# A two-layer hybrid transformer trunk: the even layer's probability-value products as f32r passes of high and low parts

## The chip, the cores and the metric

The kernel runs on one core of a Trainium2 chip. The metric is the device time of one execution in microseconds (us): 1273.81 us before, the median of 3 runs (1273.42 to 1273.93).

## What is computed

A decoder trunk of two layers over 512 tokens of width 1024, all in float32, then a final RMSNorm. Each layer is a mixer and a gated MLP, each behind an RMSNorm and with a residual. The change touches only the mixer of the even layer (layer 0), which has two head groups. Cut to what matters:

```
# A: 4 heads, each with two 64-wide q/k maps (c = 0, 1) and one 128-wide value
s = einsum('bqhcd,bkhcd->bhcqk', q * scale, k)
e, den = masked_exp(s, causal)                 # exp(s - row maximum), row sums
o = einsum('bhcqk,bkhe->bqhce', e, v) / den
o_a = o[c=0] - lam * o[c=1]                    # then an RMSNorm over the 128 values

# B: 8 heads of 64, three (window, dilation) branches combined by their softmax sums;
# here as one softmax in which every key is weighted by the number of branches that see it
o_b = einsum('bhqk,bkhd->bqhd', e * count, v) / sum(e * count)
```

The 1024 columns of o_a and o_b together go into one output projection.

## The kernel before, in words

**Number format of the large products.** A float32 operand is split in a high part of type f32r (a rounded copy, made by ScalarE) and a low part (the operand minus the high part, made by VectorE or GpSimd), and a product is three f32r passes: high by high, high by low, low by high. The weights come in 101 tiles of 128x2048, two buffers (`w_raw`, `w_hi`, `w_lo`); each is loaded by SyncE, copied to `w_hi` by ScalarE (L369), and its `w_lo` is made by VectorE (L773) in the even mixer and by GpSimd (L290) after it.

**The even mixer** runs in 8 groups: g = 0 to 3 are the A heads (a loop), g = 4 to 7 are pairs of B heads (unrolled). The 384 columns of q, k and v of a group lie in `y` (part of the buffer `region`), the value in the last 128 of them. A group has 8 units k = 0 to 7: `i = k // 2` is the block of 128 queries, `m = k % 2` the map or head, and `w = 128 * (i + 1)` the number of keys. A unit passes through four engines:

- TensorE: scores into PSUM bank m (L1421 and L1422, f32r, then a mask, L1424 or L1426);
- VectorE: the negated row maximum (`max_unit`, L881);
- ScalarE: exp into `probs` (`exp_unit`, L491 or L494), which lies in `xn`;
- VectorE, in B only: the weights of the keys and their sum (`weigh_unit`, L887);
- TensorE: transposes of 128x128 into PSUM bank 2 + m (`turn_probs`, L1392);
- ScalarE: the copy into `probsT` (`copy_turned`, L502), also in `xn`;
- TensorE: the product with the values (`values`, L1408), i + 1 float32 matmuls of 128 columns in A and 64 in B, into bank 6 or 7;
- VectorE: after two units, division by the sums and the way out (`heads_out`: L893 to L900 in A, L893 and L904 in B).

**The order** is written out by hand, and each engine runs its instructions in that order. Iteration k of `attention_ab` on TensorE holds: scores of unit k, a piece of the projection of the next group (`part`, L1365, 12 matmuls of 384 columns; for k = 0 and 2 to 7 and at the end of the group, none at k = 1 and 8), transposes of unit k - 1, values of unit k - 2. At k = 9 stand the transposes of the next group's q and k (L1355), then the values of unit 7. In group 7 there is no next group: pieces of the output projection (L1332) stand in iterations 0, 2, 3, 4, 5 and 7. VectorE runs, in iteration k: maximum of unit k; at k = 4, 6, 8 `heads_out`; from k = 4 to 7 an addition to the next group's q, k, v (`add_part`, L856); in B `weigh_unit`; at k = 1 a whole weight tile's low part (L773), and at k = 5 another; in groups 4 to 6, at the end of some iterations, `between`, which holds the A heads' norm (`sub_norm`, four L1088). After iteration 8 it makes the low parts of the next q and k (`head_lows`, L840 and L843) and runs the last `heads_out`. GpSimd rotates q and k of the next group (L314 to L320).

Of the kernel before, what the change touches and what calls it, by code (L numbers as in the profile page):

```python
# [21 lines left out]
NT = SEQ // 128  # L22
# [31 lines left out]
def trunk_program(nc, x_in, weights, consts, masks, vectors, gains, out):  # L54
# [5 lines left out]
    with ExitStack() as ctx:  # L60
# [28 lines left out]

        xn = sb("xn", [128, 2, DM])  # L90
        probs = xn[:, 0, :].rearrange("p (a n) -> p a n", a=2)
# [41 lines left out]
        first_lo = nc.alloc_sbuf_tensor_at("first_lo", [128, 4, SEQ], f32r, offset=region_at + 4 * (12288 + 4 * SEQ))  # L133
        masks_f32 = region[:, 12288:12288 + M_END]
        split_at = region_at + 4 * (12288 + M_END)
# [21 lines left out]
        pT_ready, pT_copied, pv_ready, o_ready = sem("pT_ready"), sem("pT_copied"), sem("pv_ready"), sem("o_ready")  # L157
        conv_started, conv_done, silu_ready = [[sem(f"{n}{l}") for l in range(2)] for n in
# [204 lines left out]
        def _(sc):  # L363
# [133 lines left out]
            def copy_turned(g, k):  # L497
# [4 lines left out]
                sc.activation(probsT[:, m, 0:w], ps[:, 2 + m, 0:w], ACT.Copy).then_inc(pT_copied, 1)  # L502

            def attention_ab(kind, g, more):

                for k in range(9):
                    if k == 0 and more:
                        copy_low(g + 1, 1, 5)
                    if k < 8:
                        exp_unit(kind, g, k)  # L510
                    if k >= 1:
                        copy_turned(g, k - 1)
# [23 lines left out]
            def attention_c(h, g):  # L536
# [5 lines left out]
                for k in range(9):  # L542
# [4 lines left out]
                    if k >= 1:  # L547
                        copy_turned(g, k - 1)
# [189 lines left out]
        def _(ve):  # L738
# [138 lines left out]

            def max_unit(g, k):
# [11 lines left out]
            def heads_out(kind, h, g, i):  # L890
# [12 lines left out]
                elif kind == "B":  # L903
                    ve.tensor_tensor(y[:, i, ds(384 * g, 128)].rearrange("p (m d) -> p m d", m=2),  # L904
                                     bank[:, 0:128].rearrange("p (m d) -> p m d", m=2),
                                     rden[:, 2 * i:2 * i + 2].unsqueeze(2).broadcast_to([128, 2, 64]),
                                     ALU.mult).then_inc(o_ready, 1)
# [288 lines left out]
        def _(pe):  # L1196
# [186 lines left out]
            def turn_probs(kind, g, k):  # L1383
# [5 lines left out]
                if k >= 2:  # L1389
                    pe.wait_ge(pT_copied, 8 * g + k - 1)  # L1390
# [462 lines left out]
```

## Time and profile before

| | |
|---|---|
| median of 3 runs | 1273.81 us (1273.42 to 1273.93) |
| the profiled execution, its own time | 1273.91 us |
| its span in the trace | 1272.1 us |
| busy share of TensorE (matmul), VectorE, ScalarE, GpSimd | 97%, 40%, 39%, 45% |
| granted clock of TensorE, mean | 0.998 of 2.4 GHz |

The profiled execution is 1.8 us longer than its span, which is what lies around the span, and 0.1 us above the median. The even mixer's attention groups run from 44 to about 280 us. In the profile, PE is TensorE's matmul side and PEld its weight loads; a group starts with the first `L1421` matmul of 128 columns. These starts lie at 44.02, 73.20, 102.53, 131.88, 161.22, 192.09, 221.63 and 252.50 us, so that an A group takes 29.3 us and a B group 29.5 to 30.9 us. A float32 matmul shows as two records in the trace, an f32r or bf16 matmul or a transpose as one.

### The profile page before, as it was taken

Reading aid. Unit: us, or ns where it says so; the run is one execution under the profiler, and the core shown is the slowest. Engines: PE = TensorE matmul, PEld = TensorE weight load, DVE = VectorE, ACT = ScalarE, POOL = GpSimd, SP = SyncE. Lnnn points to the kernel's source line nnn. Section 1 sums busy time; section 2 is a strip of 40 time slices with the busy share of each in tenths; the row PEclk is TensorE's granted clock in tenths of the full one; section 3 lists DMA queues with packets and bytes.
Section 4 is the critical chain, followed back from the end, with each engine's and each line's share of the span. In section 5 each row is a group of like instructions: output and inputs, shape, how many; then the busy total and the mean of one; then the engine's idle time right before and its main releaser. Section 6 shows DMA issues by size and latency. Waiting matters only on the chain.

```text
span 1272.1 us, 17211 instructions
## 1 busy us (share of the span) xinstructions
PE 1232.1 (97%) x6376; PEld 1055.9 (83%) x6376; DVE 506.2 (40%) x885; ACT 494.0 (39%) x702; POOL 566.6 (45%) x501
## 2 busy tenths in 40 slices
PE   5999999999999999999999999999999999999996
PEld 5999989888888888888878879878888888888885
DVE  6665577755212112132324165634522121222324
ACT  4455545544323222243334255443523232343332
POOL 1344444414344444466644441611444444456662
PEclk9999999999999999999999999999999999999999
DMA  7221111112222222222223211210222222222221
GB/s 267 94 81 66 66 67 67 67 67 83 100 99 99 99 99 92 98 75 99 99 99 102 81 67 67 99 67 34 86 97 98 99 99 99 99 99 98 87 80 66
DMA packets 17036, 114.75 MB, mean 90 GB/s; under 512 B 1888, under 2 KB 2016, under 8 KB 4064
## 3 DMA queue, kind: packets, MB, share of 16 engines
q1 hardware_dynamic: 16128, 110.99, 23.9%
q10 hardware_dynamic: 864, 3.15, 0.8%
q8 instruction: 31, 0.51, 0.2%
q14 instruction: 13, 0.11, 0.0%
HBM read 112.03 MB, written 2.10 MB: 90 GB/s over the span
## 4 chain that ended last, share of the span: by engine, by line
issue 38%; POOL 30%; PE 24%; DVE 5%; ACT 2%; DMA 1%; POOLq 0%; DVEq 0%; ACTq 0%
POOL w_lo L290 30%; PE ps L1365 7%; PE ps L1633 2%; PE ps L1277 2%; PE ps L1408 2%; PE ps L1613 2%; PE ps L1557 2%; PE ps L1243 1%; PE ps L1392 1%; DVE w_lo L773 1%; PE ps L1287 1%; PE ps L1355 1%; PE ps L1258 1%; PE ps L1696 1%; ACT tmp L419 1%
## 5 line engine op out<-in xcount | busy, mean ns | idle before, releaser
L290 POOL TENSOR_TENSOR w_lo<-w_raw,w_hi 128x512 fp32r<-128x512 f32 (+1 forms) x326 | 457.3, 1434 | 535.5 <-ACT w_hi L369 476.6
L369 ACT ACTIVATE w_hi<-w_raw 128x2048 fp32r<-128x2048 f32 x96 | 183.7, 1913 | 313.7 <-PE ps L1287 155.2
L1287 PE MATMUL ps<-hT_hi,w_hi 128*128 128x512 f32 x688 | 267.7, 389 | 0.0
L1287 PE MATMUL ps<-hT_hi,w_lo 128*128 128x512 f32 x688 | 267.7, 389 | 0.0
L1287 PE MATMUL ps<-hT_lo,w_hi 128*128 128x512 f32 x688 | 267.6, 389 | 0.0
L1287 PEld LDWEIGHTS ps<-hT_lo,w_hi 128*128 128x128 f32 x688 | 129.2, 188 | 27.0
L1287 PEld LDWEIGHTS ps<-hT_hi,w_lo 128*128 128x128 f32 x688 | 129.2, 188 | 26.8
L1287 PEld LDWEIGHTS ps<-hT_hi,w_hi 128*128 128x128 f32 x688 | 129.2, 188 | 26.4
L1002 DVE TENSOR_TENSOR hT_lo<-region,hT_hi 128x2048 fp32r<-128x2048 f32 (+1 forms) x22 | 58.5, 2668 | 144.4 <-ACT hT_hi L584 144.4
L972 DVE SCALAR_TENSOR_TENSOR qk<-ps,vec,qk 128x511 f32<-128x511 f32 x44 | 33.0, 750 | 202.9 <-ACT qk L558 202.9
L558 ACT ACTIVATE qk<-ps,vec 128x512 f32<-128x512 f32 x44 | 34.3, 780 | 178.4 <-PE ps L1287 166.3
L1527 PE MATMUL ps<-w_hi,hT_hi 128*128 128x512 f32 x256 | 99.6, 389 | 0.0
L1527 PE MATMUL ps<-w_lo,hT_hi 128*128 128x512 f32 x256 | 99.6, 389 | 0.0
L1527 PE MATMUL ps<-w_hi,hT_lo 128*128 128x512 f32 x256 | 99.6, 389 | 0.0
L982 DVE TENSOR_TENSOR region<-ps,qk 128x512 f32 (+1 forms) x44 | 30.4, 691 | 155.4 <-PE ps L1287 155.4
L314 POOL TENSOR_TENSOR tmp<-region,cst 128x256 f32<-128x256 f32 x30 | 23.4, 780 | 143.5 <-DVE region L856 115.8
L1365 PE MATMUL ps<-w_hi,hT_hi 128*128 128x384 f32 x224 | 80.6, 360 | 1.4 <-ACT region L483 1.0
L1365 PE MATMUL ps<-w_hi,hT_lo 128*128 128x384 f32 x224 | 75.2, 336 | 0.0
L1365 PE MATMUL ps<-w_lo,hT_hi 128*128 128x384 f32 x224 | 74.0, 335 | 0.4 <-DVE w_lo L773 0.4
L881 DVE TENSOR_REDUCE neg_max<-ps 128x1 f32<-128x128 f32 (+3 forms) x80 | 39.1, 489 | 44.0 <-PE ps L1426 20.8
L1527 PEld LDWEIGHTS ps<-w_lo,hT_hi 128*128 128x128 f32 x256 | 48.1, 188 | 10.0
L1527 PEld LDWEIGHTS ps<-w_hi,hT_hi 128*128 128x128 f32 x256 | 48.1, 188 | 10.0
(212 smaller groups left out, 2194.7 us busy)
## 6 DMA issues: line engine op xcount, KB each, us to landing
w_raw<-weights SPq DMA_DIRECT2D x101, 1024.0 KB, 4.8
gain<-gains ACTq DMA_DIRECT2D x5, 512.0 KB, 3.6
out<-region SPq DMA_DIRECT2D x4, 512.0 KB, 2.6
x<-x_in SPq DMA_DIRECT2D x3, 512.0 KB, 10.9
cst<-consts SPq DMA_DIRECT2D x1, 640.0 KB, 12.7
x<-x_in ACTq DMA_DIRECT2D x1, 512.0 KB, 6.6
region<-masks SPq DMA_DIRECT2D x1, 384.0 KB, 13.3
vec<-vectors SPq DMA_DIRECT2D x1, 282.5 KB, 12.9
```

The lines of the kernel that those rows point to most:

```text
L290: ins = pool.tensor_tensor(w_lo[:, slot, cols], w_raw[:, slot, cols], w_hi[:, slot, cols].bitcast(f32), ALU.subtract)
L369: sc.activation(w_hi[:, slot, :], w_raw[:, slot, :], ACT.Copy).then_inc(w_hi_ready, 1)
L558: sc.activation(qk[:, s, :], ps[:, s, :], ACT.Identity, scale=vec[:, ds(8 * i + (col + 2), 1)], bias=vec[:, ds(8 * i + (col + 3), 1)]).the ...
L881: ve.tensor_reduce(neg_max[:, k:k + 1], ps[:, m, 0:w], AX.X, ALU.max, negate=True).then_inc(max_ready, 1)
L972: own.link(ve.scalar_tensor_tensor(qk[:, s, 1:SEQ], ps[:, s, 0:SEQ - 1], vec[:, ds(8 * i + (col + 1), 1)], qk[:, s, 1:SEQ], ALU.mult, ALU. ...
L982: ve.tensor_tensor(act[:, ds(2 * i + s, 1), :], ps[:, 2 + s:3 + s, :], qk[:, 2 + s:3 + s, :], ALU.mult).then_inc(val_bank_free[l], 1)
L1002: ve.tensor_tensor(hT_lo[:, places, :], act[:, ds(kt, count), :], hT_hi[:, places, :].bitcast(f32), ALU.subtract).then_inc(act_lo[l], count)
L1277: ins = pe.matmul(ps[:, banks[t], 0:width], h[:, k0 + k, t * 128:(t + 1) * 128], w[:, slot, k * width:(k + 1) * width], start=first and k ...
L1287: ins = pe.matmul(bank, w[:, slot, k * pitch + 128 * s:k * pitch + 128 * s + 128], h[:, k:k + 1, :], start=k == 0 and n == 0, stop=k == KT ...
L1365: ins = pe.matmul(ps[:, bank, 0:384], h_[:, 4 * half + k, t * 128:(t + 1) * 128], w_[:, half, k * 384:(k + 1) * 384], start=first and k == ...
L1408: ins = pe.matmul(o, probsT[:, m, b * 128:(b + 1) * 128], v, start=b == 0, stop=b == i)
L1527: ins = pe.matmul(ps[:, 4 * c + t, :], a[:, t * 128:(t + 1) * 128], w[:, slot, u * 512:(u + 1) * 512], start=first and u == units[0] and n ...
```

## The change

In groups 0 to 7 the transposed probabilities and the values are split in high and low parts, and their product runs as f32r matmuls:

- ScalarE copies a group's values to the high half of a new buffer `v_split` (`value_highs`, one instruction of 512 columns after the exp of unit 0). VectorE makes the low half (`value_lows`, one instruction of 512 columns) in iteration 1, ahead of the weight tile.
- ScalarE's copy of the transposed probabilities goes to `probsT_hi`, of type f32r, in the same place and with the same length. VectorE makes `probsT_lo` (`low_turned`) from PSUM and `probsT_hi`, one instruction of w columns for each unit: unit k - 2 in iteration k behind `max_unit`, and unit 7 ahead of `head_lows`. It lies in `stage`.
- In A, a block takes three matmuls of 128 columns in place of one float32 matmul. In B it takes one of 128 columns (high probabilities by high and low values, side by side) and one of 64 (low by high), in place of one float32 matmul of 64.
- In B, `heads_out` multiplies both halves by the inverse sums and adds them: three instructions for one, each behind the one before.
- The values of unit k - 2 now wait for `pT_low` (the low part) and no longer for `pT_copied`; those of unit 0 also for `v_ready`. The transposes of unit k wait for the low part of unit k - 2.
- `q_split`, `k_high` and `k_low` move up by 256 columns to make room.

```diff
+            def value_highs(g):
+
+                v = y[:, :, ds(384 * g + 256, 128)].rearrange("p t (m d) -> p t m d", m=2)
+                sc.activation(v_split[:, :, :, 0, :], v, ACT.Copy).then_inc(v_high, 1)
...
                     if k < 8:
                         exp_unit(kind, g, k)
+                    if k == 0:
+                        value_highs(g)
...
+            def value_lows(g):
+
+                v = y[:, :, ds(384 * g + 256, 128)].rearrange("p t (m d) -> p t m d", m=2)
+                ve.wait_ge(v_high, g + 1)
+                ve.tensor_tensor(v_split[:, :, :, 1, :], v, v_split[:, :, :, 0, :].bitcast(f32), ALU.subtract)\
+                  .then_inc(v_ready, 1)
...
+                    o = y[:, i, ds(384 * g, 128)].rearrange("p (m d) -> p m d", m=2)
+                    both = bank[:, 0:256].rearrange("p (m h d) -> p m h d", m=2, h=2)
+                    r = rden[:, 2 * i:2 * i + 2].unsqueeze(2).broadcast_to([128, 2, 64])
+                    low = o_tmp[:, :].rearrange("p (m d) -> p m d", m=2)
+                    own.link(ve.tensor_tensor(low, both[:, :, 1, :], r, ALU.mult))
+                    own.link(ve.tensor_tensor(o, both[:, :, 0, :], r, ALU.mult))
+                    ve.tensor_tensor(o, o, low, ALU.add).then_inc(o_ready, 1)
...
+            def low_turned(g, k):
+                i, m, w = unit(k)
+                ve.wait_ge(pT_copied, 8 * g + k + 1)
+                ve.tensor_tensor(probsT_lo[:, m, 0:w], ps[:, 2 + m, 0:w], probsT_hi[:, m, 0:w].bitcast(f32),
+                                 ALU.subtract).then_inc(pT_low, 1)
...
                     if k < 8:
                         max_unit(g, k)
+                    if k >= 2:
+                        low_turned(g, k - 2)
...
                     if k == 1:
+                        value_lows(g)
                         split_lo(2 * g + 3, 1)
...
+                low_turned(g, 7)
...
+                    pe.wait_ge(pT_low, 8 * g + k + 1)
+                    if k == 0:
+                        pe.wait_ge(v_ready, g + 1)
...
                     if kind == "A":
-                        v, o = y[:, b, ds(384 * g + 256, 128)], ps[:, 6 + i % 2, 128 * m:128 * m + 128]
...
+                        pe.matmul(o, hi, v_split[:, b, :, 0, :], start=b == 0, stop=False)
+                        pe.matmul(o, hi, v_split[:, b, :, 1, :], start=False, stop=False)
+                        ins = pe.matmul(o, lo, v_split[:, b, :, 0, :], start=False, stop=b == i)
+                        continue
+                    if kind == "B":
+                        pe.matmul(o, hi, v_split[:, b, m, :, :], start=b == 0, stop=False)
+                        ins = pe.matmul(o[:, 0:64], lo, v_split[:, b, m, 0, :], start=False, stop=b == i)
+                        continue
```

TensorE, group 0, iteration 2, from the transpose of unit 1 to the scores of unit 3. `xn` holds the probabilities, `cst` the identity. Before:

```order
L1392 MATMUL ps<-cst,xn 128x128
L1408 ISA
L1408 MATMUL ps<-region,xn 128x128
```

After:

```order
L1426 MATMUL ps<-cst,xn 128x128
L1436 REGISTER_ALU
L1443 MATMUL ps<-v_split,probsT_hi 128x128
L1444 MATMUL ps<-v_split,probsT_hi 128x128
L1445 MATMUL ps<-v_split,probsT_lo 128x128
```

One float32 matmul became three f32r matmuls, at the same place in the row.

VectorE, the start of an A group (the maxima of units 0 and 1, the weight tile of iteration 1, the maximum of unit 2). Before:

```order
L881 TENSOR_REDUCE neg_max<-ps 128x1
L880 REGISTER_ALU
L881 TENSOR_REDUCE neg_max<-ps 128x1
L772 ISA
L773 TENSOR_TENSOR w_lo<-w_raw,w_hi 128x2048
L880 REGISTER_ALU
L881 TENSOR_REDUCE neg_max<-ps 128x1
```

After:

```order
L902 TENSOR_REDUCE neg_max<-ps 128x1
L895 REGISTER_ALU
L896 ISA
L896 TENSOR_TENSOR v_split<-region,v_split 128x8x64
L786 ISA
L787 TENSOR_TENSOR w_lo<-w_raw,w_hi 128x2048
L901 REGISTER_ALU
L902 TENSOR_REDUCE neg_max<-ps 128x1
L941 TENSOR_TENSOR probsT_lo<-ps,probsT_hi 128x128
```

(The after piece starts with the maximum of unit 1.) The low part of unit 0, for which TensorE's first values wait, stands behind the value lows, the weight tile and the maximum of unit 2.

VectorE, a B group, from the weight tile of iteration 5 to the addition of iteration 6. Before:

```order
L773 TENSOR_TENSOR w_lo<-w_raw,w_hi 128x2048
L881 TENSOR_REDUCE neg_max<-ps 128x1
L893 RECIPROCAL rden<-den 128x2
L904 TENSOR_TENSOR region<-ps,rden 128x128
L856 TENSOR_TENSOR region<-region,ps 128x384
```

After:

```order
L787 TENSOR_TENSOR w_lo<-w_raw,w_hi 128x2048
L902 TENSOR_REDUCE neg_max<-ps 128x1
L941 TENSOR_TENSOR probsT_lo<-ps,probsT_hi 128x384
L914 RECIPROCAL rden<-den 128x2
L929 TENSOR_TENSOR o_tmp<-ps,rden 128x128
L930 TENSOR_TENSOR region<-ps,rden 128x128
L931 TENSOR_TENSOR region<-region,o_tmp 128x128
L870 TENSOR_TENSOR region<-region,ps 128x384
```

Three instructions more stand in this iteration ahead of the addition and of `weigh_unit`.

## Rows read from the trace of the kernel before

**Rows 1.** The page: busy time of engines; then tenths in 40 slices.

```profile
PE 1232.1 (97%) x6376; PEld 1055.9 (83%) x6376; DVE 506.2 (40%) x885; ACT 494.0 (39%) x702; POOL 566.6 (45%) x501
...
DVE  6665577755212112132324165634522121222324
```

**Rows 2.** Stretches of one A and one B group: length, busy time by engine.

```profile
103.00:134.00 31.00, 30.40 (x203) 28.78 (x203) 19.14 (x43) 16.58 (x36) 12.84 (x20) 1.00 0.18 68
...
192.00:219.00 27.00, 26.58 (x178) 24.69 (x177) 20.01 (x47) 12.09 (x23) 14.46 (x20) 1.00 0.22 79
```

**Rows 3.** Timeline, PE: start, duration; values of unit 6, then what follows; A, B.

```profile
97.14 1.06 PE L1408 MATMUL ps<-region,xn 128*128 x8
98.04 1.15 PE L1355 MATMUL ps<-cst,qk 128*128 128x128 f32 x9
...
216.01 1.00 PE L1408 MATMUL ps<-region,xn 128*128 128x64 f32 x8
216.85 1.15 PE L1355 MATMUL ps<-cst,qk 128*128 128x128 f32 x9
```

**Rows 4.** Timeline, group 0: f32r scores of 128 columns, and a weight load (PEld).

```profile
46.88 0.22 PE L1421 MATMUL ps<-k_high,q_split 128*128 128x128 f32 x1
46.94 0.27 PE L1422 MATMUL ps<-k_low,q_split 128*128 128x128 f32 x1
47.05 0.23 PE L1426 MATMUL ps<-mask_bf,ident_bf 128*128 128x128 bf16 x1
...
46.88 0.19 PEld L1422 LDWEIGHTS ps<-k_low,q_split 128*128 128x128 f32 x1
```

**Rows 5.** Timeline, group 1, iterations 0 to 2: DVE, ACT and PE.

```profile
76.03 0.29 DVE L881 TENSOR_REDUCE neg_max<-ps 128x1 f32<-128x128 f32 x1 [0.19 <-PE ps L1426]
76.24 2.28 DVE L773 TENSOR_TENSOR w_lo<-w_raw,w_hi 128x2048 fp32r<-128x2048 f32 x1
78.44 0.42 DVE L881 TENSOR_REDUCE neg_max<-ps 128x1 f32<-128x256 f32 x1
...
76.36 0.37 ACT L494 ACTIVATE xn<-ps,neg_max 128x128 f32<-128x128 f32 x1
...
76.39 0.33 PE L1392 MATMUL ps<-cst,xn 128*128 128x128 f32 x1 [0.39 <-ACT xn L494]
...
79.11 0.39 PE L1408 MATMUL ps<-region,xn 128*128 x2
```

**Rows 6.** Durations: ACT copy and DVE operations of 512, 512, 384 and 128 columns.

```profile
L502 ACT ACTIVATE xn<-ps 128x512 f32<-128x512 f32 x12 | 7.2, 598 | 8.8 <-PE ps L1392 8.8
...
L843 DVE TENSOR_TENSOR k_low<-ps,k_high 128x512 fp32r<-128x512 f32 x4 | 2.8, 692 | 0.1
L856 DVE TENSOR_TENSOR region<-region,ps 128x384 f32<-128x384 f32 x12 | 6.5, 544 | 0.0
L904 DVE TENSOR_TENSOR region<-ps,rden 128x128 f32<-128x128 f32 x10 | 2.9, 291 | 0.3
```

**Rows 7.** Timeline, group 4, iteration 1 and 2: the weight tile and the values of unit 0.

```profile
165.31 2.29 DVE L773 TENSOR_TENSOR w_lo<-w_raw,w_hi 128x2048 fp32r<-128x2048 f32 x1
...
167.26 0.33 PE L1408 MATMUL ps<-region,xn 128*128 128x64 f32 x2
```

**Rows 8.** Timeline, group 4, iterations 6 to 8: the norm, its followers, TensorE.

```profile
183.80 0.68 DVE L881 TENSOR_REDUCE neg_max<-ps 128x1 f32<-128x512 f32 x1
...
184.49 0.78 PE L1408 MATMUL ps<-region,xn 128*128 128x64 f32 x6
186.46 0.66 PE L1392 MATMUL ps<-cst,xn 128*128 128x128 f32 x4 [1.19 <-DVE xn L887]
```

**Rows 9.** Timeline, group 5, end of iteration 7: the norm of 128x128, four times.

```profile
214.66 2.47 DVE L1088 SCALAR_TENSOR_TENSOR region<-region,rstd,sub_gain 128x128 f32<-128x128 f32 x4
217.06 0.15 DVE L893 RECIPROCAL rden<-den 128x2 f32<-128x2 f32 x1
```

**Rows 10.** Timeline, group 7: iteration 6, then iteration 8 and 9.

```profile
271.79 0.69 DVE L881 TENSOR_REDUCE neg_max<-ps 128x1 f32<-128x512 f32 x1 [1.22 <-PE ps L1424]
271.92 0.78 PE L1408 MATMUL ps<-region,xn 128*128 128x64 f32 x6
277.57 1.96 PE L1408 MATMUL ps<-region,xn 128*128 128x64 f32 x16
277.77 0.60 ACT L502 ACTIVATE xn<-ps 128x512 f32<-128x512 f32 x1 [0.46 <-PE ps L1392]
```

**Rows 11.** Waits of PE from 67 to 162 us: in total, times, longest.

```profile
PE ps L1392 <- ACT xn L494: 1.2, 3, 0.4
```

More of the change, by code:

```diff
@@ L133, in trunk_program @@
         first_lo = nc.alloc_sbuf_tensor_at("first_lo", [128, 4, SEQ], f32r, offset=region_at + 4 * (12288 + 4 * SEQ))
+        probsT_hi = nc.alloc_sbuf_tensor_at("probsT_hi", [128, 2, SEQ], f32r, offset=xn_at + 4 * DM)
+        probsT_lo = nc.alloc_sbuf_tensor_at("probsT_lo", [128, 2, SEQ], f32r, offset=stage_at)
         masks_f32 = region[:, 12288:12288 + M_END]
-        split_at = region_at + 4 * (12288 + M_END)
+        v_split = nc.alloc_sbuf_tensor_at("v_split", [128, NT, 2, 2, 64], f32r, offset=region_at + 4 * 12288)
+        split_at = region_at + 4 * (12288 + 1024)
         q_split, k_high, k_low = (nc.alloc_sbuf_tensor_at(n, [128, 2, SEQ], f32r, offset=split_at + 4 * 2 * SEQ * j)
@@ L501, in copy_turned @@
                     sc.wait_ge(pv_ready, 8 * g + k - 1)
-                sc.activation(probsT[:, m, 0:w], ps[:, 2 + m, 0:w], ACT.Copy).then_inc(pT_copied, 1)
+                dst = probsT if kind == "C" else probsT_hi
+                sc.activation(dst[:, m, 0:w], ps[:, 2 + m, 0:w], ACT.Copy).then_inc(pT_copied, 1)
+            def value_highs(g):
+                v = y[:, :, ds(384 * g + 256, 128)].rearrange("p t (m d) -> p t m d", m=2)
+                sc.activation(v_split[:, :, :, 0, :], v, ACT.Copy).then_inc(v_high, 1)
             def attention_ab(kind, g, more):
@@ L547, in attention_c @@
                     if k >= 1:
[L548 removed]
+                        copy_turned("C", g, k - 1)
             def mlp(l, n0):
@@ L1389, in turn_probs @@
                 if k >= 2:
-                    pe.wait_ge(pT_copied, 8 * g + k - 1)
+                    pe.wait_ge(*((pT_copied, 8 * g + k - 1) if kind == "C" else (pT_low, 8 * g + k - 1)))
                 for b in range(i + 1):
@@ L1396, in values @@
                 i, m, w = unit(k)
-                pe.wait_ge(pT_copied, 8 * g + k + 1)
+                if kind == "C":
+                    pe.wait_ge(pT_copied, 8 * g + k + 1)
+                else:
+                    pe.wait_ge(pT_low, 8 * g + k + 1)
+                    if k == 0:
+                        pe.wait_ge(v_ready, g + 1)
                 if i >= 2 and m == 0:
                     pe.wait_ge(o_ready, 4 * g + i - 1)
+                o = ps[:, 6 + i % 2, 128 * m:128 * m + 128]
                 for b in range(i + 1):
+                    hi, lo = (p[:, m, b * 128:(b + 1) * 128] for p in (probsT_hi, probsT_lo))
                     if kind == "A":
-                        v, o = y[:, b, ds(384 * g + 256, 128)], ps[:, 6 + i % 2, 128 * m:128 * m + 128]
-                    elif kind == "B":
-                        v, o = y[:, b, ds(384 * g + (256 + 64 * m), 64)], ps[:, 6 + i % 2, 64 * m:64 * m + 64]
+                        pe.matmul(o, hi, v_split[:, b, :, 0, :], start=b == 0, stop=False)
[6 more added lines that the diff above has]
+                        continue
                     else:
```

11 lines of the change are left out of this document (5 added, 6 removed).

## The prediction, made before the result

> **What bounds the kernel now.** I read the page's busy shares first, then its 40 slices, then the timelines of single groups. TensorE is busy 97% of the span; VectorE is busy 40% on average, but 6 to 7 tenths in slices 1 to 9, which are the attention groups this change touches [rows 1]. A 31 us stretch of the A groups has 19.1 us of VectorE work, a 27 us stretch of B has 20.0 us [rows 2]. So TensorE sets the time, and VectorE has over a third of its time free in A and a quarter in B. The question is then twofold: how long the new value products are on TensorE, and whether a low part from VectorE is there when TensorE comes to the values. Where it isn't, TensorE waits, since nothing else stands in its row.
>
> **TensorE, A groups.** Each of the 80 blocks (4 groups, 20 blocks each) has one float32 matmul, two records, and gets three f32r matmuls. The 8 records of unit 6 start at 97.14 and what follows starts at 98.04, which is 0.90/8 = 0.11 us a record [rows 3]. What does an f32r matmul of 128 columns take? The trace has no long run of them. It has pairs: the first starts at 46.88, the second at 46.94, the mask's at 47.05 [rows 4]. The first follows in 0.06 us and has its weights loaded already; the second takes 0.11 us, and its weight load starts only at 46.88, with the first matmul. In B, a float32 record has half the columns (64) and still takes (216.85 - 216.01)/8 = 0.105 us [rows 3]. A record that doesn't shrink with its columns is bound by something that every record has, and that is the weight load. All new matmuls load weights of 128x128, so I take 0.11 us for each, with 0.085 (the mean of the pair, 0.17/2) and 0.06 as the cheaper bounds. A: 240 x 0.11 - 160 x 0.11 = +8.8 us.
>
> **TensorE, B groups.** 80 blocks had two records and get two f32r matmuls (128 and 64 columns). 160 x 0.11 - 160 x 0.105 = +0.8 us; I take +0.5, since the narrow ones may keep 0.105.
>
> The Trainium skill, in "TensorE: Matmul & The Clock Gate", section "Back-to-back issue gap", gives about 81 ns a matmul of 128 columns in a stream with weight loads. That speaks against my 0.11, and by it A would be 240 x 0.081 - 17.6 = +1.8 and B 160 x 0.081 - 16.8 = -3.8, a TensorE sum of -2.0 in place of +9.3. No row here shows a run at that rate.
>
> **What of it is given back.** At the start of groups 1 to 4 TensorE waits 0.4 to 0.5 us for the first exp or its weighting, since VectorE is still busy with the last `heads_out` (0.39 in group 1, 1.2 in all for three groups) [rows 5, 11]. The longer values of unit 7 (12 records for 8, +0.44) lie ahead of this wait and fill it: -1.6 us for four groups. TensorE's sum is +8.8 + 0.5 - 1.6 = +7.7 us.
>
> **The first values of each group.** This is the largest wait that the change adds. In iteration 1 VectorE ran the maximum of unit 1 (76.03), the weight tile (76.24) and the maximum of unit 2 (78.44) [rows 5]. Now, in group 1: ScalarE, free at 76.36 where it started the second exp, makes the value highs first (0.62 us, by the copy of 512 columns at 0.60) and is done at about 77.0 [rows 5, 6]. VectorE waits for that, makes the value lows until 77.6 (0.60 from start to start, by the 0.69 of `k_low` less 0.08 of overlap), the weight tile until 79.8 (2.2), the maximum of unit 2 until 80.2, then the low part of unit 0 (0.29) [rows 6]: ready at 80.5. TensorE used to start these values at 79.11 [rows 5]. It waits 1.4 us. The second exp comes 0.6 us later, but its transposes stand behind a `part` of 2.1 us, which hides that. In B it is the same with other numbers: the tile started at 165.31, the value lows push it to 165.9, so the low part is there at 168.8, against values at 167.26 [rows 7]: 1.5 us. There are 4 x 1.4 + 4 x 1.5 = +11.6 us. This wait can't be less than 0.8 us a group (no value lows in the way, 6.4 us in all) unless VectorE does the low part ahead of the tile, which its order excludes.
>
> **Later values of A.** Behind a `part` of 2.1 us the low part (maximum 0.6 and low 0.6 at most) is hidden. Iteration 8 has no `part`: the values of unit 6 stand behind one set of transposes (0.45) and the longer values of unit 5, and need copy plus low part, 0.60 + 0.69. I take 0.1 a group, +0.5 us.
>
> **Later values of B.** VectorE gets, from k = 4 to the weighting of unit 7, low parts of 256, 256, 384 and 384 columns (0.35 + 0.35 + 0.47 + 0.47) and two `heads_out` that have three chained instructions for one of 0.29 (+0.7 each) [rows 6]: 3.0 us of work. The groups have about 2 us of idle VectorE there, partly ahead of the tile of k = 5. What doesn't fit shows on TensorE:
> - Group 4: the norm ends at 183.80, then come the maximum and the low part of unit 5 (0.6 + 0.56), ready at 185.0 even with no lag, against values at 184.49; TensorE waits 1.19 us already for the weighting of unit 7 [rows 8], and that comes 1.6 us later. +1.7 us for the two.
> - Group 5: the norm of 2.47 us at the end of iteration 7 delayed nobody before. Now the low part of unit 6 stands behind it: 217.06 + 0.69 + 0.05 = 217.8, against values at 216.01 [rows 3, 9]. That is 1.8 us; with 0.8 of lag carried over, +2.6 us.
> - Group 6: iteration 8 alone, +0.5 us.
> - Group 7: iteration 6 has no piece of projection. The maximum of unit 6 starts at 271.79, so the low part of unit 4 is ready at about 273.0, against 271.92: 1.05 us. In iteration 8 and 9 the last 16 records ran without a gap from 277.57, while the copy of unit 7 started at 277.77 [rows 10]; now VectorE's low part of unit 6, a `heads_out`, an addition and the low part of unit 7 (0.61 + 1.1 + 0.6 + 0.69) stand in the way, 0.5 + 1.4 us. +3.0 us.
>
> That is +7.8 us for B.
>
> ScalarE's part adds nothing beyond the above: its copies keep their length, and the value highs are counted. SyncE, GpSimd and the DMAs issue what they did before; what stands behind the attention is shifted as a whole.
>
> **Sum.** 7.7 + 11.6 + 0.5 + 7.8 = +27.6 us on the profiled execution's 1273.9 (0.1 above the median): **1301.5 us**, 2.2% slower.
>
> **Rivals.**
> - *Cheap f32r matmuls.* If a record takes the pair's mean of 0.085, A loses 240 x 0.025 = 6.0 us of its cost, B 160 x 0.025 = 4.0 us, of which TensorE returns some by waiting longer for the same low parts (half in B, I estimate): -8.0, so 1293.5 us. For it: the pair. Against it: the 0.11 of the second and of the records of 64 columns. The skill's 81 ns would come out about here too.
> - *VectorE becomes the bound of B.* A B group of 27 us has 20.0 us of VectorE work; the change adds 3.7 (low parts), 0.6 and 4 x 0.7, which is 27.1. If its chained waits don't overlap with TensorE's pieces at all, groups 4 to 7 each lose 3 us more: 1313 us.
> - *The low parts are hidden.* Then only TensorE's records count: 1273.9 + 7.7 = 1281.6 us. It needs VectorE to be 1.4 us ahead in iteration 2, and the start at 78.44 right behind the tile says it is not.
> - *Faster than before.* If f32r records ran at 0.06, as the first of the pair does, A is 240 x 0.06 - 17.6 = -3.2 and B 160 x 0.06 - 16.8 = -7.2, together -10.4 us: 1263.5 us. It decides for faster only if all new waits together stay under 10 us, and I count 19.9.
> - *It does nothing measurable.* The new work would have to fall where TensorE idles; it idles 0.39 us ahead of the first transposes of an A group [rows 5], against 2.2 us of new records in it.
>
> **Chances.** Forecast (1296 to 1308) 0.64; cheap matmuls 0.15; VectorE-bound B 0.12; low parts hidden 0.05; faster 0.02; no change 0.02. The range goes from 1290 (cheap matmuls with their bound) to 1311 (most of the VectorE case). A measurement of this kernel tells about 0.2%, 2.5 us, from no change. So faster 0.02, same 0.02, slower 0.96.
>
> **What would show it.** Right: A groups about 32 us from start to start (29.3 before) and B groups 31 to 34; TensorE idle ahead of the first values of every group by 1.4 to 1.5 us, released by the low part; 0.11 us between starts of value records, 80 records more in all. VectorE at 8 tenths or more in the slices of the B groups, and in group 5 the low part of unit 6 right behind the norm. Wrong: no idle ahead of values in iteration 2, value records at 0.06 to 0.09 us, or waits in A in iterations 3 to 7, where I have none.

## The result, and the profile after

The changed kernel takes 1306.26 us (median of 4 runs, 1305.94 to 1308.97), against 1273.62 us of the kernel before: a ratio of 1.026, 95% interval 1.025 to 1.028. It is 32.6 us slower. The forecast was 1301.5 us, in a range from 1290 to 1311. The profiled execution of the changed kernel took 1308.97 us with a span of 1307.2, which is 35.1 us more than the span before. So what follows explains 35.1 us for the profile, and 32.6 for the median.

The page of the changed kernel, against [rows 1]; `PEclk` is the granted clock in tenths of 2.4 GHz, in 40 slices of 32.7 us:

```profile
PE 1252.3 (96%) x6452; PEld 1072.3 (82%) x6456; DVE 544.7 (42%) x989; ACT 498.3 (38%) x710; POOL 566.0 (43%) x501
...
DVE  6766677786521212132325046644522222232324
...
PEclk9999998899999999999999999999999999999999
```

TensorE has about the 80 records more that the change makes (6452 for 6376; a few records can be missing from a trace), VectorE 38.5 us more work, and two slices show an 8 where the kernel before had a 9 in all 40. The span grew by 35 us, TensorE's busy time by 20. The rest is waiting, and TensorE's waits over the whole span name its releaser (waited for: us in total, times, longest):

```profile
PE ps L1448 <- DVE probsT_lo L941: 12.4, 13, 1.8
PE ps L1443 <- DVE probsT_lo L941: 5.0, 4, 1.3
...
PE ps L1338 <- DVE region L870: 1.5, 1, 1.5
```

L941 is `low_turned`, L1443 and L1448 are the first value matmuls of a block in A and in B: 17.4 us in 17 waits, none of which the kernel before had. This is the mechanism of the forecast. Here is its first place, group 1, where [rows 5] showed the kernel before (DVE, then PE):

```profile
79.90 0.69 DVE L896 TENSOR_TENSOR v_split<-region,v_split 128x512 fp32r<-128x512 f32 x1 [0.23 <-ACT v_split L514]
80.50 2.29 DVE L787 TENSOR_TENSOR w_lo<-w_raw,w_hi 128x2048 fp32r<-128x2048 f32 x1
82.71 0.42 DVE L902 TENSOR_REDUCE neg_max<-ps 128x1 f32<-128x256 f32 x1
83.04 0.28 DVE L941 TENSOR_TENSOR probsT_lo<-ps,probsT_hi 128x128 fp32r<-128x128 f32 x1
...
83.45 0.32 PE L1443 MATMUL ps<-v_split,probsT_hi 128*128 128x128 f32 x1 [1.29 <-DVE probsT_lo L941]
83.61 0.27 PE L1444 MATMUL ps<-v_split,probsT_hi 128*128 128x128 f32 x1
83.72 0.27 PE L1445 MATMUL ps<-v_split,probsT_lo 128*128 128x128 f32 x1
83.83 0.33 PE L1467 MATMUL ps<-k_high,q_split 128*128 128x256 f32 x1
```

Value lows, weight tile, maximum, low part: four instructions in a row without a gap, and TensorE idle for 1.29 us until the last of them ends. The second and third value matmul start 0.11 us apart, where [rows 3] had 0.11 for a float32 record. The delay is longer than the idle time shown: the scores of unit 3 (83.83) start 7.29 us after the group's start here and 5.76 us after it in the run of the TensorE half below, which has the same records and no such wait. That is 1.53 us for a wait of 1.29.

Not all of it is waiting. The profile shows four stretches in which the granted clock is low. These are windows of the changed kernel (length, busy time of PE, PEld, DVE, ACT and POOL, then the granted clock as a share of 2.4 GHz, DMA share, GB/s):

```profile
202.00:208.00 6.00, 6.00 (x37) 5.82 (x37) 3.66 (x9) 3.36 (x7) 2.34 (x5) 0.72 0.00 0
216.00:222.00 6.00, 5.42 (x24) 5.00 (x24) 3.06 (x12) 1.78 (x6) 0.00 (x0) 0.72 0.46 175
240.00:248.00 8.00, 8.00 (x39) 8.00 (x39) 4.53 (x11) 4.55 (x6) 0.03 (x1) 0.57 0.00 1
312.00:318.00 6.00, 5.91 (x29) 5.52 (x30) 3.15 (x8) 1.79 (x3) 0.00 (x0) 0.72 0.00 0
```

In their middle, windows of 2 us show 0.50, the lower of the two levels, 1.2 GHz. The clock takes 6 x 0.28 us three times and 8 x 0.43 us once there, 8.5 us, if all of TensorE's work in them is stretched by it. In the kernel before, no window of 2 us between 44 and 280 us was under 0.99. One such place on PE, the end of group 5:

```profile
239.99 0.24 PE L1449 MATMUL ps<-v_split,probsT_lo 128*128 128x64 f32 x1
240.07 1.85 PE L1389 MATMUL ps<-cst,qk 128*128 128x128 f32 x12
241.57 0.46 PE L1448 MATMUL ps<-v_split,probsT_hi 128*128 128x128 f32 x1
241.82 0.36 PE L1449 MATMUL ps<-v_split,probsT_lo 128*128 128x64 f32 x1
242.00 0.45 PE L1448 MATMUL ps<-v_split,probsT_hi 128*128 128x128 f32 x1
```

A pair of value matmuls takes 0.43 us there (241.57 to 242.00), twice the 0.22 us of the pairs before 240. The clock fell about 2 us after the end of the longest wait of the group, 1.80 us ahead of 239.16: the window from 241 to 242 us is the first under 1.00, with 0.57.

The starts of groups 0 to 7 are now at 43.75, 76.54, 109.14, 141.71, 174.28, 209.33, 247.26 and 281.65 us, and the output projection that follows group 7 begins at 319.70 (284.37 before):

| group | before, us | after, us | more | of it at low clock | left | forecast |
|---|---|---|---|---|---|---|
| 0 to 3 (A), sum | 117.2 | 130.5 | 13.3 | 0 | 13.3 | 13.7 |
| 4 | 30.9 | 35.1 | 4.2 | 1.7 | 2.5 | 2.8 |
| 5 | 29.5 | 37.9 | 8.4 | 5.1 | 3.3 | 4.1 |
| 6 | 30.9 | 34.4 | 3.5 | 0 | 3.5 | 2.0 |
| 7 | 31.9 | 38.1 | 6.2 | 1.7 | 4.5 | 4.5 |

(The column "forecast" splits its 27.6 us by group. The 0.5 us for B's records is left out of it. The group starts are 0.3 us earlier than before, so the column "more" adds up to 35.6 us, and "left" to 27.1.)

### The profile page after: what moved, and what is told of

Its sections match the earlier page's. It is cut to its first block, busy times and chain, and to the rows that moved or that the text cites. A ratio compares the mean times of both kernels' runs of the same rounds, so it can differ in the third digit from the quotient of the medians.

```text
span 1307.2 us, 17487 instructions
## 1 busy us (share of the span) xinstructions
PE 1252.3 (96%) x6452; PEld 1072.3 (82%) x6456; DVE 544.7 (42%) x989; ACT 498.3 (38%) x710; POOL 566.0 (43%) x501
## 4 chain that ended last, share of the span: by engine, by line
issue 37%; POOL 29%; PE 22%; DVE 7%; ACT 3%; DMA 0%; POOLq 0%; DVEq 0%; ACTq 0%
POOL w_lo L296 29%; PE ps L1399 6%; DVE w_lo L787 2%; PE ps L1679 2%; PE ps L1311 2%; PE ps L1659 2%; PE ps L1603 1%; PE ps L1277 1%; PE ps L1389 1%; PE ps L1321 1%; PE ps L1426 1%; PE ps L1292 1%; DVE neg_max L902 1%; ACT tmp L425 1%; PE ps L1443 1%
## 5 line engine op out<-in xcount | busy, mean ns | idle before, releaser
L1321 PEld LDWEIGHTS ps<-hT_hi,w_hi 128*128 128x128 f32 x688 | 129.2, 188 | 26.6
L320 POOL TENSOR_TENSOR tmp<-region,cst 128x256 f32<-128x256 f32 x30 | 24.8, 828 | 172.9 <-DVE region L870 145.4
## 6 DMA issues: line engine op xcount, KB each, us to landing
region<-masks SPq DMA_DIRECT2D x1, 384.0 KB, 13.3
```

What stands on the lines that cost most here:

```text
L1321: ins = pe.matmul(bank, w[:, slot, k * pitch + 128 * s:k * pitch + 128 * s + 128], h[:, k:k + 1, :], start=k == 0 and n == 0, stop=k == KT ...
```

## The experiments

Two theories were tested. **Theory 1** is the forecast's: TensorE pays for 80 more records and waits for low parts that stand too far back in VectorE's row. **Theory 2** was formed on the result: the idle stretches of TensorE make the chip grant the half clock for a few microseconds afterwards, which costs time on top of the idle time itself. The kernel before was run beside each set: 1273.4 us with the first four runs, 1274.2 with the next four, 1273.8 with the last two.

### One half of the change at a time

TensorE's half: the same f32r matmuls, all on high parts, with no low part made or waited for.

```diff
-                    pe.wait_ge(pT_low, 8 * g + k + 1)
+                    pe.wait_ge(pT_copied, 8 * g + k + 1)
...
-                        pe.matmul(o, hi, v_split[:, b, :, 1, :], start=False, stop=False)
+                        pe.matmul(o, hi, v_split[:, b, :, 0, :], start=False, stop=False)
...
-                    if k >= 2:
-                        low_turned(g, k - 2)
```

> The TensorE half of the change alone: the value products run as the same number of f32r matmuls of the same shapes (three of 128 columns in A, one of 128 and one of 64 in B), but all on high parts; VectorE makes no low parts of probabilities or values and takes B's output in one instruction as before, and TensorE waits for ScalarE's copy only. Left out of the computation: every low part of these products. Theory 1 (a record costs 0.11 us, given by the weight load; 7.7 us net): 1281 us (1279 to 1284), granted clock 0.998 as before, no wait at the values. Rival (the pair's mean, 0.085 us a record): 1272 to 1274 us. Rival on the whole result (f32r value products are what costs 33 us, by whatever way): near 1306 us.

Measured: 1281.2 us (1279.6 to 1282.6), ratio 1.006 (1.004 to 1.007). Theory 1's 1281 is met; 0.085 us a record is out. Its A groups take 30.8 us, 1.5 more than before (group 0: 1.9), and groups 5 and 6 take 29.5 and 30.9, exactly as before: B's records cost nothing. What it doesn't show as expected is the clock. In the profiled execution the wait of group 4 that the kernel before has as well [rows 8] is followed by a low stretch (PE, and a window):

```profile
191.95 0.66 PE L1419 MATMUL ps<-cst,xn 128*128 128x128 f32 x4 [1.26 <-DVE xn L908]
...
192.00:202.00 10.00, 10.00 (x53) 10.00 (x54) 3.73 (x9) 5.95 (x10) 1.75 (x4) 0.66 0.01 2
```

That is 3.4 us lost. By their mean clock two of its four executions had it (0.995, 1282.5 and 1282.6 us; the former is the profiled one), two had not (0.998 and 0.997, 1279.6 and 1279.9). So the half as such is worth about 6 us, and the clock adds 3 in some executions.

VectorE's and ScalarE's half: all low parts and the longer B output are made, but the product is the float32 one and doesn't wait for them.

```diff
-                dst = probsT if kind == "C" else probsT_hi
+                dst = probsT
...
-                    pe.wait_ge(pT_low, 8 * g + k + 1)
+                    pe.wait_ge(pT_copied, 8 * g + k + 1)
...
-                        pe.matmul(o, hi, v_split[:, b, m, :, :], start=b == 0, stop=False)
-                        ins = pe.matmul(o[:, 0:64], lo, v_split[:, b, m, 0, :], start=False, stop=b == i)
+                        v, o = y[:, b, ds(384 * g + (256 + 64 * m), 64)], ps[:, 6 + i % 2, 128 * m:128 * m + 64]
...
+                        pe.wait_ge(pT_low, 8 * g + 7)
                         turn_qk(g + 1)
```

> The VectorE and ScalarE half alone: low parts of probabilities and values are made at the same places, B's output takes its three instructions, but the product is the float32 one of before and doesn't wait for a low part (only the transposes that overwrite a PSUM bank do, two units later, and the next group's q and k transposes do for unit 6). The output takes the float32 product and so has a wrong low half added in B. Theory 1 (what costs is that TensorE's values wait for the low part): little of the 33 us shows, 1276 to 1281 us, from maxima, weights and q/k transposes that come later in B, clock near 0.998. Rival (VectorE as such is the bound, with or without that wait): 1290 us or more.

Measured: 1282.1 us, ratio 1.007 (1.005 to 1.009), 1 us above the expected range and far from the rival's 1290. The two halves cost 7.8 and 8.7 us, 16.5 together, and the whole costs 32.9. Half of the cost is in neither of them: it is in the wait that joins them and in the clock. VectorE's half alone still delays TensorE a little in several places (between 44 and 330 us; the first row is the transposes, waiting for B's weighting, the second a `part` whose weight tile comes later, the third a wait for the low part ahead of the next group's transposes, added for this run):

```profile
PE ps L1426 <- DVE xn L908: 2.4, 3, 1.5
PE ps L1399 <- DVE w_lo L787: 2.3, 6, 0.7
...
PE ps L1389 <- DVE probsT_lo L941: 1.1, 1, 1.1
```

### Weight loads or columns

The TensorE half again, with an A block as one matmul of 256 columns and one of 128, so that 384 columns are streamed with two weight loads and not three.

```diff
-                        pe.matmul(o, hi, v_split[:, b, :, 0, :], start=b == 0, stop=False)
-                        pe.matmul(o, hi, v_split[:, b, :, 0, :], start=False, stop=False)
-                        ins = pe.matmul(o, lo, v_split[:, b, :, 0, :], start=False, stop=b == i)
+                        o = ps[:, 6 + i % 2, 256 * m:256 * m + 256]
+                        both = v_split[:, b:b + 1, :, 0, :].broadcast_to([128, 2, 2, 64])
+                        pe.matmul(o, hi, both, start=b == 0, stop=False)
+                        ins = pe.matmul(o[:, 0:128], lo, v_split[:, b, :, 0, :], start=False, stop=b == i)
```

> As the run of the TensorE half alone (no low parts, no wait for them), but an A block takes two f32r matmuls in place of three: one of 256 columns and one of 128. The columns streamed are the same 384; only the number of records, and so of weight loads, falls by 80, to that of the kernel before. Left out: all low parts. Theory 1 (a record costs its weight load, 0.11 us, up to about 200 columns): the cost in A goes away, 1274 to 1277 us against 1281 with three. Rival (the columns or the type cost, not the records): 1280 to 1282 us.

Measured: 1274.7 us (10 runs), ratio 1.0007 (0.9997 to 1.0017): no difference from the kernel before. Its A groups take 29.2 to 29.4 us. Five of the executions, at a mean clock of 0.997 or 0.998, took 1273.7 to 1274.3 us; the other five, at 0.996, took 1275.1 to 1276.1. The profiled one is among the latter, and its clock falls at 187.6 us, behind the wait of group 4 that the kernel before has too. So at full clock nothing is left of the 6 us. The columns and the type cost nothing, the 80 records did. PE, group 0, values of unit 6, then PEld, the weight loads of these matmuls:

```profile
67.74 0.33 PE L1438 MATMUL ps<-v_split,probsT_hi 128*128 128x256 f32 x1
67.91 0.22 PE L1439 MATMUL ps<-v_split,probsT_hi 128*128 128x128 f32 x1
67.97 0.34 PE L1438 MATMUL ps<-v_split,probsT_hi 128*128 128x256 f32 x1
68.14 0.23 PE L1439 MATMUL ps<-v_split,probsT_hi 128*128 128x128 f32 x1
...
67.69 0.19 PEld L1438 LDWEIGHTS ps<-v_split,probsT_hi 128*128 128x128 f32 x1
67.79 0.19 PEld L1439 LDWEIGHTS ps<-v_split,probsT_hi 128*128 128x128 f32 x1
67.92 0.19 PEld L1438 LDWEIGHTS ps<-v_split,probsT_hi 128*128 128x128 f32 x1
68.02 0.19 PEld L1439 LDWEIGHTS ps<-v_split,probsT_hi 128*128 128x128 f32 x1
```

A pair takes 0.23 us (67.74 to 67.97), as two float32 records did; three f32r matmuls of 128 columns took 0.33. Note that the 128-column matmul is followed after 0.06 us, as the first of the pair in [rows 4] was, and the 256-column one after 0.17. The weight loads start 0.10 to 0.13 us apart whatever the columns, and 0.11 apart in the changed kernel too (97.26, 97.37, 97.48 us and so on, in group 1): their spacing, and not the columns, gives the 0.23 of a pair. A start-to-start time of one matmul says little here; the sum over a repeated pattern does. A fixed cost of a matmul other than its weight load would look the same, and no run tells the two apart. Nor does a run show at how many columns the columns begin to count; the 384 of a `part` matmul take 0.17 us.

### The wait at the first values

The whole change, with the low part of unit 0 ahead of the weight tile.

```diff
-                    if k >= 2:
+                    if k >= 3:
                         low_turned(g, k - 2)
...
                         value_lows(g)
+                        low_turned(g, 0)
                         split_lo(2 * g + 3, 1)
```

> The whole change, but in each group the low part of unit 0 is made ahead of the weight tile of iteration 1, not behind it and the maximum of unit 2. Nothing is left out. Theory 1: the wait of 1.2 to 1.8 us at the first values is gone in all 8 groups (10.9 us in the changed kernel's trace), and 2 us come back elsewhere since the tile ends later: about 9 us less, 1297 us; and if such waits are what takes the clock down in B, some of the four stretches at 1.2 GHz go as well, 1291 to 1297 us. Rival (VectorE has no time for it, the wait only moves): within 3 us of 1306.

Measured: 1298.3 us (1295.6 to 1299.1), ratio 1.019 (1.018 to 1.021): 8 us faster than the change. Theory 1 had about 9, and 1291 to 1297 us, so the result is 1 us above its range and outside the rival's, within 3 us of 1306. The waits for L941 fell from 17.4 to 5.9 us, all of them in B, and 3.5 us came back as the wait for the weight tile that now ends later:

```profile
PE ps L1449 <- DVE probsT_lo L941: 5.9, 7, 1.9
PE ps L1400 <- DVE w_lo L787: 3.5, 7, 0.9
```

Three low stretches remained, with 5.1 us lost; the run without most of that clock loss (0.996) took 1295.6 us, those at 0.992 1299.0.

### The norms

The whole change, with two norms of the A heads moved to where no low part of unit 5 or 6 stands behind them.

```diff
-            between = {4: {3: lambda: refine(0, 16), 6: lambda: sub_norm(0)}, 5: {3: lambda: sub_norm(1), 7: lambda: sub_norm(2)},
+            between = {4: {3: lambda: refine(0, 16), 8: lambda: sub_norm(0)}, 5: {3: lambda: sub_norm(1), 8: lambda: sub_norm(2)},
```

> The whole change, with two of the four norms of the A heads moved on VectorE: from the end of iteration 6 of group 4 and of iteration 7 of group 5 to the end of iteration 8 of the same groups, so that the low parts of units 5 and 6 no longer stand behind them. Nothing is left out. Theory 1: the wait of 1.8 us in group 5 and of 1.0 us in group 4 fall to 0.5 us each, and with the former the longest stretch at 1.2 GHz (7 us, 3.4 lost) may go: 1300 to 1305 us. Rival (the norm only pushes the next group's q/k low parts or first maxima): within 1 us of 1306.

Measured: 1306.1 us (1304.4 to 1306.3). The rival's number came, though not by its way. In the profiled execution (1304.4 us) groups 4 and 5 take 33.5 us each (35.1 and 37.9 in the change), 6.0 us less together: 5.1 of it is the clock, which didn't fall there, and 0.9 the waits. The 1.80 us ahead of unit 6's values in group 5 became 0.34, with 0.73 ahead of unit 7's. But the end of group 7 had a longer stretch at half clock, from 306 to 313 us, 3.4 us lost, where the change had lost 1.7. The other three executions had a lower mean clock still (0.993) and took 1.7 us more. At equal clock little is left of the gain: 1306.0 to 1306.3 us at 0.993 here, 1306.5 us at 0.993 in the change.

Both orders together:

> The whole change with both orders: the low part of unit 0 ahead of the weight tile (as in the run that made it 8 us faster), and the two norms at the end of iteration 8. Nothing is left out. Theory 1: the two gains add where they are apart, 1291 to 1296 us, still far above 1273.4, since TensorE's records (+6 to +8 us) and B's VectorE work stay.

Measured: 1295.3 us (1294.5 to 1297.3), ratio 1.017 (1.015 to 1.019): within the range, 3 us below the run with the low part alone, and 21 us above the kernel before. One low stretch remained in its profile.

### The clock

The whole change with work in the waits of B: bf16 matmuls of constants into an unused part of the PSUM bank, placed in TensorE's row ahead of the values that wait longest.

```diff
+                fill = 0 if kind != "B" else {(4, 5): 7, (5, 6): 13, (7, 4): 6, (7, 7): 8}.get((g, k), 9 if k == 0 else 0)
+                for _ in range(fill):
+                    pe.matmul(ps[:, 6 + i % 2, 256:512], ident_bf[:, :], mask_bf[:, M_DIL:M_DIL + 256], start=True, stop=True)
```

> The whole change, with bf16 matmuls of 256 columns of constants into an unused part of the PSUM bank put in TensorE's row in the B groups, ahead of the values that wait 1 us or more: 9 ahead of unit 0 of groups 4 to 7, 7 ahead of unit 5 of group 4, 13 ahead of unit 6 of group 5, 6 and 8 ahead of units 4 and 7 of group 7. They fill the waits with work and shorten none. Theory 2 (TensorE's idle stretches make the chip grant half the clock, four stretches with 8.5 us lost): the clock stays at 1.0 throughout, and the time falls to 1297 to 1301 us although work was added. Rival (the clock falls for another reason, or costs nothing because TensorE waits anyway): 1306 us or more.

Measured: 1302.0 us (1301.0 to 1302.7), 4 us less than the change, with 70 matmuls more, and 1 us above the range that theory 2 gave. No window of 2 us under 0.99 is left in the attention of the profiled execution; three of the four executions had a mean clock of 0.998, the slowest 0.996. Windows of this kernel around three of the four places where the clock fell in the change:

```profile
200.00:214.00 14.00, 13.54 (x98) 12.61 (x97) 11.02 (x28) 8.40 (x15) 4.11 (x7) 1.00 0.00 1
214.00:224.00 10.00, 9.10 (x60) 8.04 (x59) 7.65 (x23) 4.53 (x8) 1.48 (x3) 1.00 0.26 105
236.00:252.00 16.00, 14.81 (x106) 14.01 (x105) 12.36 (x33) 7.58 (x15) 1.80 (x4) 1.00 0.11 36
```

Groups 4 and 5 take 33.6 and 33.5 us (35.1 and 37.9). So theory 2 holds: the fall of the clock comes from TensorE's idle stretches, and what the clock cost can be had back by useless work. From the start of group 4 to the output projection the profiled executions differ by 7.9 us (145.4 and 137.5), close to the 8.5 at stake. As wholes they differ by 7.0 (1308.97 and 1301.96), the medians by 4.3: the other three executions of the change had a mean clock of 0.993 or 0.994 and had lost less.

Is it idleness alone, or idleness together with the small f32r matmuls? The changed kernel with all its waits and float32 products:

```diff
-                dst = probsT if kind == "C" else probsT_hi
+                dst = probsT
...
-                        pe.matmul(o, hi, v_split[:, b, m, :, :], start=b == 0, stop=False)
-                        ins = pe.matmul(o[:, 0:64], lo, v_split[:, b, m, 0, :], start=False, stop=b == i)
+                        v, o = y[:, b, ds(384 * g + (256 + 64 * m), 64)], ps[:, 6 + i % 2, 128 * m:128 * m + 64]
```

> The changed kernel with all its VectorE and ScalarE work and with the values still waiting for their low part, but the product itself the float32 one of before. It leaves the low parts out of the product, and B's low half is wrong. It tells two theories of the clock apart. Theory 2a (TensorE's idle stretches alone take the clock down): waits are those of the changed kernel, so four or so stretches at 1.2 GHz appear, clock 0.992 to 0.995, and the time is 1306 less the 6 us of new records in A: 1299 to 1301 us. Theory 2b (it takes idle stretches together with the small f32r matmuls, which stream 64 or 128 columns of one pass for each weight load where a float32 record streams two passes' worth): the clock stays at 0.998, and the time is 1291 to 1295 us.

Measured: 1301.7 us (1299.1 to 1303.8), at a clock of 0.993 to 0.997; theory 2a had 1299 to 1301, theory 2b 1291 to 1295. Low stretches appear with float32 products too (two in the profile, 1.7 us lost in each), so the waits are enough without f32r value products, as theory 2a had it. The faster executions have the higher clock: 0.997 at 1299.1, 0.996 at 1301.3, 0.993 at 1302.2 and 1303.8. TensorE waited for L941 19.0 us in this kernel, more than in the change, since shorter records arrive earlier:

```profile
PE ps L1447 <- DVE probsT_lo L941: 19.0, 21, 1.8
```

It also shows that the terms don't add: with the waits in place, f32r records cost 4 to 5 us and not 7.8. In the A groups, where no clock falls, they cost 0.9 us a group (32.6 against 31.7), where they cost 1.5 without the waits. That the low stretches are fewer here than in the change could be the type or chance; the runs don't settle it.

The best order and the matmuls of constants together:

> The low part of unit 0 ahead of the weight tile, and bf16 matmuls of constants in the four waits of B that remain (7 ahead of unit 5 of group 4, 13 ahead of unit 6 of group 5, 6 and 8 ahead of units 4 and 7 of group 7). Nothing is left out. Theory 2: the three low-clock stretches of the run without filler (4.5 us lost) go, 1293 to 1295 us at a clock of 0.998. Rival: no change against 1298, or slower by the filler.

Measured: 1293.0 us (1292.6 to 1293.3), the best form of the whole change that was run, and the steadiest: all four executions at 0.997, none of them slower than 1293.3, and no low stretch in the attention of the profiled one. It is theory 2's 1293 to 1295. It is still 1.5% slower than the kernel before.

### TensorE's records against VectorE's time in A

The best form with the wide A product, whose high and low results lie in separate columns and are added by VectorE.

```diff
+                    own.link(ve.tensor_scalar(o_sum[:, :], bank[:, 384:512], rden[:, 2 * i + 1:2 * i + 2], neg_lam[:, :],
+                                              ALU.mult, ALU.mult))
+                    own.link(ve.scalar_tensor_tensor(o_sum[:, :], bank[:, 128:256], rden[:, 2 * i:2 * i + 1],
+                                                     o_sum[:, :], ALU.mult, ALU.add))
...
+                    own.link(ve.tensor_tensor(o, o, o_sum[:, :], ALU.add))
```

> The whole change in the best form so far (low part of unit 0 first, matmuls of constants in four waits of B) with A's product as one matmul of 256 and one of 128 columns, and so with high and low results in separate columns that VectorE adds in the A groups: three instructions more in each of 16 outputs. Nothing is left out. If VectorE has room in A (20 of 31 us busy before), it gains TensorE's 4 to 6 us, 1287 to 1289 us. If the longer output pushes maxima and low parts in A, as in B, it gives the gain back or more: 1293 to 1300 us. I hold the second for likelier.

Measured: 1306.1 us (1305.7 to 1306.3), clock 0.998. It loses 13 us against the run before, where TensorE had 6 to gain, and is 6 us above the worse of the two expected ranges. A groups take 34.2 to 35.2 us (31.6 without), and TensorE waits for `add_part` (L871), which now stands behind the longer output, before it may reuse a bank:

```profile
PE ps L1406 <- DVE region L871: 9.0, 8, 1.5
PE ps L1454 <- DVE probsT_lo L947: 4.8, 8, 0.9
...
103.00:134.00 31.00, 27.37 (x177) 25.50 (x178) 22.88 (x52) 15.26 (x34) 10.24 (x16) 1.00 0.13 38
```

VectorE is busy 22.9 of 31 us here, 19.1 in [rows 2]: a quarter of it is free, and it still sets the pace, as TensorE's waits for it show. That this is so because its instructions are chained and stand in one row is argued, not tested.

## Why the prediction was right, and where it was not

The direction and the mechanism came as forecast: the value records on TensorE, and its waits for low parts that stand too far back in VectorE's row. The terms follow one by one.

- **TensorE's records, +7.7 us.** Measured by themselves: 7.8 us in the median, of which about 1.5 is clock, so 6. The 0.11 us a record is right (three in 0.33 us), and its reason is borne out as far as the runs go: with two records for the same columns the cost is gone, and the weight loads start 0.11 us apart. What was given back in A was more than forecast: 1.5 us more a group, not 1.8, since the wait for ScalarE's copy ahead of a `part` (0.22 us in group 1) was filled as well. B: +0.5 forecast, nothing measured in groups 5 and 6.
- **The rate in the Trainium skill.** The Trainium skill, in "TensorE: Matmul & The Clock Gate", section "Back-to-back issue gap", has about 81 ns a matmul of 128 columns. Here a run of f32r matmuls took 111 ns each, three in 0.33 us; the measurement decides, and the rate of that section doesn't hold for the f32r matmuls of this kernel. The time of a weight load on the same page of the Trainium skill, section "LDWEIGHTS (loading the stationary operand)", its columns by 1.2 GHz, gives an estimate of 107 ns for 128. That is close to the distance between the starts of two loads here, 0.11 us, but not to the length of one load's row, 0.19 us.
- **The wait at the first values, +11.6 us.** Measured 1.29 us at most in A (5.0 in all for four groups) and 1.47, 1.76, 1.76 and 1.18 in B: 11.2 us of idle time. The delay is larger where it can be read, 1.53 us in group 1. Taking it away gave 8 us, as 3.5 came back for the tile.
- **Later values in A, +0.5 us.** No wait is shown there, but from the scores of unit 7 to the next group's start group 1 takes 10.93 us, against 10.67 in the run of the TensorE half: 0.26 us a group, 1.0 in all. With 1.5 and 1.53 that makes up the 3.3 us by which an A group grew.
- **Later values in B, +7.8 us.** In group 4 0.27 and 1.01 us, and 0.22 for the weighting, where the kernel before had waited 1.19 us; in group 5 0.20 us and 1.80 us, the latter right behind the norm as forecast; in group 6 0.23 and 0.34; in group 7 0.92, 0.33 and 1.17. Here is group 5, to be set beside [rows 9] (DVE, then PE):

```profile
236.03 2.47 DVE L1122 SCALAR_TENSOR_TENSOR region<-region,rstd,sub_gain 128x128 f32<-128x128 f32 x4
238.43 0.68 DVE L941 TENSOR_TENSOR probsT_lo<-ps,probsT_hi 128x512 fp32r<-128x512 f32 x1
...
239.16 0.33 PE L1448 MATMUL ps<-v_split,probsT_hi 128*128 128x128 f32 x1 [1.80 <-DVE probsT_lo L941]
```

  The norm itself is long there. In the kernel before, a norm of the same shape takes 1.13 us while GpSimd stands idle (DVE, early in group 5), and 2.47 in [rows 9], where GpSimd rotates the next q and k. No run tested whether GpSimd's work is what doubles it.

```profile
200.69 1.13 DVE L1088 SCALAR_TENSOR_TENSOR region<-region,rstd,sub_gain 128x128 f32<-128x128 f32 x4
```

  Group 6 was forecast too low, 2.0 against 3.5: the transposes of the A heads for the output (L1338) wait for the additions of the next q, k and v, 1.5 us where it was 0.9, and that step wasn't in the sum.
- **The clock, not in the sum.** This is the term that failed: 8.5 us in the profiled execution. The forecast took TensorE's waits at their length. Without the clock the profile gives 35.1 - 8.5 = 26.6 us against 27.6 forecast, so the steps add up, in part because single misses cancel (records 1.7 us too high, group 6 1.5 us too low). The distance from 1301.5 to the median of 1306.3 is of the clock's size: at mean clocks of 0.993 and 0.994, against 0.998 before, some 5 to 6 us were lost, an estimate from these shares and the span. The range held it by its upper end, which had been set for another rival, and that is luck.
- **The rivals.** Cheap f32r matmuls: out, by the run of the TensorE half. VectorE as the bound of B: out as an account of the whole, since its half alone costs 8.7 us; but the run with a longer A output shows how near that is. Low parts hidden: out. Faster: even with TensorE's half at no cost the kernel would only have been level. Nothing measurable: out, by the ratio of 1.026 (1.025 to 1.028).
- **The signs.** A groups of 32.6 us, 0.11 us a record, the wait ahead of the first values in all 8 groups and no waits in iterations 3 to 7 of A came as forecast. Three signs did not. That wait was 1.14 to 1.29 us in A and 1.18 to 1.76 in B, not 1.4 to 1.5. The B groups took 34.4 to 38.1 us, and 32.8 to 36.4 without the clock, not 31 to 34; group 7 was 31.9 before, and the sum's own 4.5 for it was above that sign. And VectorE is at 8 tenths in one slice of the B groups only (7, 7, 7, 8 and 6, from the sixth slice on). The reading of VectorE before was off as well: slices 1 to 9 in [rows 1] show 5 to 7 tenths, not 6 to 7.

What stays open: why an idle stretch of the same length takes the clock down in one place or execution and not in the next. The kernel before has a wait of 1.19 us and kept its clock there; the TensorE half has one of 1.26 us at the same place and, by the mean clock, lost it in two of four executions. In the profiled execution of the change, TensorE's attention has 12 waits of 1.0 us or more, and the clock fell behind 4 of them (1.01, 1.76, 1.80 and 1.17 us), but not behind 1.76 us in group 6, 1.47 in group 4 or any of the four in A.

## What to carry to other kernels

Count matmuls, not columns, where a matmul has 128 columns or fewer and loads its own 128x128 weights: here 0.11 us each in f32r, and two products of the same probabilities side by side in one matmul of 256 columns took TensorE's extra cost to nothing (though the longer VectorE output that this needs made the whole 13 us slower). Where a new step is put on another engine and the bounding engine will wait for it, read what stands ahead of it in that engine's row: one weight tile of 2.3 us ahead of a low part of 0.3 us cost 8 us over 8 groups. Price a new wait on TensorE above its length, since the clock may fall after it (here 8.5 us beside 17.4 us of waits), and try a few useless matmuls in the wait as a test: if the time falls, it was the clock.

## What the runs showed of the hardware that was not expected

Waits of 1.0 to 1.9 us on a TensorE that is busy 96% of the time were followed, in some executions, by stretches at half clock in which 1.7 or 3.4 us were lost, 8.5 us in the profiled execution beside 17.4 us of waits. The mean clock tells the executions of one kernel apart: 0.996 at 1295.6 us and 0.992 at 1299.1 for the same program. With the waits filled by matmuls of constants, 1301.0 to 1302.7 us at 0.996 to 0.998.
